# A two-model transformer stack on one core: order of the partial sums in four FFN stages, and one weight place

## The reference

```
def swiglu(x, w_gate, w_up, w_down):
    return (jax.nn.silu(x @ w_gate) * (x @ w_up)) @ w_down
...
    for l in range(DEPTH):
        h = layer_norm(ALPHA * h + 0.5 * swiglu(h, ffn1_w_gate[l], ffn1_w_up[l], ffn1_w_down[l]),
                       ln1_g[l], ln1_b[l])
...
        h = layer_norm(ALPHA * h + 0.5 * swiglu(h, ffn2_w_gate[l], ffn2_w_up[l], ffn2_w_down[l]),
                       ln3_g[l], ln3_b[l])
```

## Time and profile before

| | |
|---|---|
| timed runs, median (lowest to highest) | 1946.63 us (1946.62 to 1950.07), 3 runs |
| profiled execution, span from first to last instruction | 1945.9 us |
| its own time | not given apart from the span |
| TensorE busy | 1931.2 us, 99% |
| VectorE, ScalarE, GpSimd busy | 74%, 52%, 8% |
| DMA | 346.66 MB, mean 178 GB/s |

### The profile page before, as it was taken

How to read it: one execution, slowest core, us unless ns; L and a number is a source line. 1 busy time by engine, 2 the same in 40 slices (tenths; PEclk the granted TensorE clock), 3 DMA queues, 4 the chain that set the end, 5 groups by cost and what they waited for, 6 DMA issues and landing times.

```text
span 1945.9 us, 42335 instructions
## 1 busy us (share of the span) xinstructions
PE 1931.2 (99%) x16150; PEld 1892.7 (97%) x16150; DVE 1431.5 (74%) x2591; ACT 1019.8 (52%) x1527; POOL 152.7 (8%) x192
## 2 busy tenths in 40 slices
PE   9999999999999999999999999999999999999998
PEld 8999989999999999899999999999999999999998
DVE  6774787987588768879978874667765775667763
ACT  4443687554455447865547443665445444565443
POOL 0001123000100011320010100000000000100000
PEclk9999999999999999999999999999999999999999
DMA  7454433545454544345553665445555555435554
GB/s 265 172 197 170 166 109 112 192 174 193 156 192 172 196 164 145 109 152 194 201 191 140 235 233 183 151 149 185 193 214 177 195 202 208 152 131 195 194 213 154
DMA packets 46830, 346.66 MB, mean 178 GB/s; under 512 B 5344, under 2 KB 6416, under 8 KB 9232
## 3 DMA queue, kind: packets, MB, share of 16 engines
q1 hardware_dynamic: 44416, 335.63, 48.0%
q0 software_dynamic: 2320, 9.74, 1.6%
HBM read 344.29 MB, written 1.07 MB: 177 GB/s over the span
## 4 chain that ended last, share of the span: by engine, by line
PE 91%; DVE 4%; ACT 2%; DVEq 1%; issue 1%; DMA 0%; ACTq 0%; SPq 0%; POOL 0%
PE ps L622 22%; PE ps L623 22%; PE ps L624 22%; PE ps L639 14%; PE ps L630 2%; PE ps L631 2%; PE ps L632 2%; DVE w_lo L1996 1%; PE ps L1162 0%; DVE pj L2465 0%; DMA h<-in_hidden 0%; DVE cst L2486 0%; PE ps L1197 0%; DVE pj L2462 0%; ACT scratch L1669 0%
## 5 line engine op out<-in xcount | busy, mean ns | idle before, releaser
L1996 DVE TENSOR_TENSOR w_lo<-raw,w_hi 128x1024 fp32r<-128x1024 f32 (+1 forms) x582 | 749.3, 1313 | 151.1 <-ACT w_hi L1300 91.5
L622 PE MATMUL ps<-x_hi,w_lo 128*128 128x256 f32 (+3 forms) x2208 | 622.1, 282 | 1.5 <-DVE x_lo L2087 0.6
L624 PE MATMUL ps<-x_hi,w_hi 128*128 128x256 f32 (+3 forms) x2208 | 615.1, 279 | 0.0
L623 PE MATMUL ps<-x_lo,w_hi 128*128 128x256 f32 (+3 forms) x2208 | 614.8, 278 | 0.0
L1297 ACT ACTIVATE w_hi<-raw 128x1024 fp32r<-128x1024 f32 x454 | 466.3, 1052 | 92.5 <-PE ps L639 49.0
L622 PE MATMUL ps<-hid_hi,w_lo 128*128 128x256 f32 (+1 forms) x1536 | 431.5, 281 | 0.1
L624 PE MATMUL ps<-hid_hi,w_hi 128*128 128x256 f32 (+1 forms) x1536 | 430.2, 280 | 0.0
L623 PE MATMUL ps<-hid_lo,w_hi 128*128 128x256 f32 (+1 forms) x1536 | 429.8, 280 | 0.0
L622 PEld LDWEIGHTS ps<-x_hi,w_lo 128*128 128x128 f32 x2208 | 414.9, 188 | 6.4 <-issue 4.2
L623 PEld LDWEIGHTS ps<-x_lo,w_hi 128*128 128x128 f32 x2208 | 415.0, 188 | 0.5
L624 PEld LDWEIGHTS ps<-x_hi,w_hi 128*128 128x128 f32 x2208 | 414.6, 188 | 0.0
(11 more groups left out here) (351 smaller groups left out, 2315.3 us busy)
## 6 DMA issues: line engine op xcount, KB each, us to landing
raw<-in_w_up SPq DMA_DIRECT2D x176, 1024.0 KB, 4.8
raw<-in_w_down SPq DMA_DIRECT2D x64, 1408.0 KB, 6.0
raw<-in_w_in SPq DMA_DIRECT2D x36, 1024.0 KB, 4.8
raw<-in_w_out SPq DMA_DIRECT2D x16, 1024.0 KB, 4.8
cst<-row_copy POOLq DMA_DIRECT2D x2, 1088.0 KB, 8.5
raw<-in_w_up SPq DMA_DIRECT2D x4, 512.0 KB, 7.2
cst<-in_consts POOLq DMA_DIRECT2D x1, 1537.5 KB, 6.5
prm<-in_prm POOLq DMA_DIRECT2D x2, 690.0 KB, 7.2
```

Of the source, the lines that this page charges most:

```text
L622: mm(dst, low, xa, start=first, stop=False)
L623: mm(dst, high, xb, start=False, stop=False)
L624: return mm(dst, high, xa, start=False, stop=last)
L1996: v.tensor_tensor(dst, src, high.bitcast(F32), ALU.subtract).then_inc(lo_done, 1)
```

## The change

Three things. In the opening up stage (place OPENING) and in the loops of the second 274-column stage, chunks are summed in the order 0, 2, 4, 6, 1, 3, 5, 7. The second 274-column stage gets a place of its own, SAME_LINE_274, with pitch 8 lines, one line of offset for the high and three for the low buffer, and it sums with `three` rather than `in_pairs`. Down-projections of q = 0 and q = 2 go through the chunks of each half grouped by f modulo four. All other FFNs keep their order.

```diff
+        SAME_LINE_274 = Place(P, LINE, 3 * LINE)
+        EVENS_FIRST = (*range(0, KD, 2), *range(1, KD, 2))
+        BY_LINE = [[f for f in range(u * HALF_F, (u + 1) * HALF_F) if f % 4 == line] for u in range(2) for line in range(4)]
...
-        def level_place(T):
-            return BESIDE_258 if T == T2 else LEVEL_274
+        def level_place(T, q):
+            return BESIDE_258 if T == T2 else SAME_LINE_274 if q == 2 else LEVEL_274
...
-                if T == T1 + 2 and place is not TIGHT:
+                if T == T1 + 2 and place not in (TIGHT, SAME_LINE_274):
                     last = in_pairs(dst, high, low, xa, xb, T)
                 else:
                     step = three_beside if T == T2 + 4 else three
-                    for k in range(KD):
-                        if k in before:
-                            before[k]()
-                        last = step(dst, high[:, k, :], low[:, k, :], xa[:, k, 0:T], xb[:, k, 0:T], k == 0, k == KD - 1)
+                    for n, k in enumerate(EVENS_FIRST if place in (OPENING, SAME_LINE_274) else range(KD)):
+                        if n in before:
+                            before[n]()
+                        last = step(dst, high[:, k, :], low[:, k, :], xa[:, k, 0:T], xb[:, k, 0:T], n == 0, n == KD - 1)
...
-                            for c in range(HALF_F):
-                                f = u * HALF_F + c
-                                col = u * W_WIDE + c * P
+                            order = [f for line in BY_LINE[4 * u:4 * u + 4] for f in line]
+                            if q not in (0, 2):
+                                order = sorted(order)
+                            for f in order:
+                                col = f * P
                                 last = three(ps[:, 4 + j, 0:T], w_hi[:, j, col:col + P], w_lo[:, j, col:col + P],
-                                             ha[:, f, 0:T], hb[:, f, 0:T], f == 0, f == NF - 1)
+                                             ha[:, f, 0:T], hb[:, f, 0:T], f == 0, (u, f) == (1, order[-1]))
```

More of the change, by code:

```diff
@@ L720, in level_up @@
                 N = T + 4 if T == T2 else T + 2
-                xs, place = (plain_hi, plain_lo_of(LEVEL_NORM[norm])), level_place(T)
+                xs, place = (plain_hi, plain_lo_of(LEVEL_NORM[norm])), level_place(T, q)
                 pieces = {5: lambda: mean(norm, T)}
@@ L1503, in unit_hi @@
                     act.wait_ge(unit_used, used)
-                    hi_unit(j, u, width, level_place(T))
+                    hi_unit(j, u, width, level_place(T, q))
                 def pair(it, j, width):
@@ L2192, in pair @@
                     if width == W_NARROW:
-                        lo_unit(turn0 + it + 1, j, 0, width, level_place(T))
+                        lo_unit(turn0 + it + 1, j, 0, width, level_place(T, q))
                     if last:
@@ L2205, in pair @@
                     if width == W_NARROW:
-                        lo_unit(turn0 + it + 1, j, 1, width, level_place(T))
+                        lo_unit(turn0 + it + 1, j, 1, width, level_place(T, q))
                     if last:
```

## The result

The changed kernel takes 1953.18 us (median of 15 timed runs, 1950.54 to 1953.41) against 1947.12 us (15 runs, 1946.50 to 1950.51) for the kernel before; the ratio is 1.0021, 95% interval 1.0014 to 1.0028. It is slower by 0.2%, where the prediction had it 2.9 us faster, and the time lies outside the predicted range of 1937.8 to 1949.6 us.

A forecast was written before the change was run, and what follows sets the result against it. TensorE, busy 1931.2 of 1945.9 us, was taken as the bound, so only matmul pace counts. Opening loop 0, downs -0.3 and second 274-column stage -2.6 gave -2.9 us: median 1943.7 us, range 1937.8 to 1949.6.

The forecast's parts named there:

- Reading: Whole kernel: TensorE busy 1931.2 of 1945.9 us, touched stages full, no wait to remove; only the matmul pace can change.
- Moved place off TensorE, cost 0: Second 274-column stage: ScalarE and VectorE write the weights at pitch 128 floats instead of 160, at cost 0.
- First 274-column loop, 118.3 us: First 274-column loop, not edited: should keep its length of 118.3 us; 120.9 would mean rival 3.
- Rival 3: Both 274-column loops settle badly, first at its twin's pace (+2.6 us), second at the TIGHT row (+1.6); 1950.9 us, chance 0.11.
- Evens first in the opening loop, predicted 0: Opening up-loop, 960 matmuls: same set of weight-to-operand distances, so 0; bounds -3.6 to +1.8 us.
- rival 2: Opening loop, downs, second 274 stage: staying on the same moving line pays, together -7.9 us; 1938.8 us, chance 0.29.
- Downs one and three, predicted -0.3 us: Down-projections one and three: grouping removes most changes between even and odd distances, -0.3 us; bounds -5.3 to +0.6.
- Second 274-column stage, predicted -2.6 us: Second 274-column loop: new order leaves the slow pace 126.0 for 123.3 ns, -2.6 us; bounds -5.0 to +1.6.
- the TIGHT row: Upper bound for the second 274-column loop: three at a time in place TIGHT, 127.7 ns, +1.6 us.
- Even and odd distance: Weights loaded an even number of lines from the moving operand are cheaper: opening loop 123.7, output projection (odd) 125.6 ns.
- Rival 4: Whole change: order and place have no effect or their effects cancel; 1946.6 us, chance 0.18.
- a rule of the Trainium skill: TensorE: separate SBUF read ports for moving operand and weight load, so order and place do nothing; time stays 1946.6 us.

The follow-up runs named there:

- e1: Changed kernel with opening loop and downs one and three back in rising order, down two grouped by line; second 274-column loop 129.24 ns a matmul.
- e12: Kernel before with only the opening loop evens first and downs one and three grouped by line; 1948.40 us, ratio 1.0010.
- e5: Kernel before with opening loop shuffled, down one in steps of two, down three backwards, second 274 loop `three`, plain's low part moved two lines; opening loop 118.78 us.
- e3: Kernel before, rising order, with opening loop in TIGHT, first 274 loop in pairs at pitch 8, second `three` at LEVEL_274; second loop 127.78 ns a matmul.
- e13: Kernel before with high x moved, opening loop in pairs, second 274 loop in pairs at distance 0, all three downs backwards in each half; 1948.27 us, ratio 1.0002.
- e15: Kernel before with the three 272-column downs backwards in each half and second 274 loop in pairs at distance 0; 1948.26 us, ratio 0.9996.
- e8: Kernel before with high x moved, opening and 274 loops in rising pairs at one distance each, downs one and three backwards; opening loop 123.34 ns a matmul.
- e7: Kernel before with opening order 0,2,1,3,4,6,5,7, first 274 loop `three` at Place(8, 1, 1), plain's low part moved two lines; second loop, pairs, 127.79 ns.

## Why the prediction was wrong

**Reading.** TensorE is the bound, the touched stages are full, and the change can act only on the pace: held. No other engine moved.

**Moved place off TensorE, cost 0.** Held: 1221 and 1058 ns.

**First 274-column loop, 118.3 us.** Held: 118.41 by the timeline. Rival 3 rested on this loop falling to its twin's pace, and in the profiled execution it didn't. The loop does have both paces: it was seen at either with the same code ahead of it (before and e1). But the regrouped down one doesn't bring the slow one about (e12), and it isn't why the change lost. Rival 3's other half, the second loop settling dearer with three at a time, did happen, at +2.47 us where it had +1.6. That its time, 1950.9, is near the lower level of the result, 1950.7, is luck: the first half of its sum didn't happen, and the opening loop and the downs, at which it had nothing, cost 1.5 us.

**Evens first in the opening loop, predicted 0.** +1.03 us, inside its bounds of -3.6 to +1.8. The step that failed is "The set is the same": what was kept was the set of distances between weights and moving operand, and what changed was how often the moving line repeats, 0 to 6 times in a sum. There was no row for that. The prediction had noted that staying on a line might have an effect of its own, and gave it the wrong sign (rival 2).

**Downs one and three, predicted -0.3 us.** +0.45. Grouping was to save the changes between even and odd distances; steps of two (e5, down one) leave one change of 10, where grouping leaves three, and gave 124.93. So there was nothing to save but 0.03 ns, and grouping adds repeats, 0.44 ns.

**Second 274-column stage, predicted -2.6 us.** +2.47, beyond even the upper bound of +1.6, and five of the seven us by which the like level (1950.7) misses the forecast. This is the term that decided the sign. Two steps failed. The first is "odds are that it doesn't reproduce the slow one": the loop was given its twin's fast pace although form and place were both new. Every trace with the unchanged code ahead of it entered this loop at 127.8 or, with the moved low part, 127.2, and the fast pace never appeared there. The second is the bound: the TIGHT row, 127.7, was taken as the worst place for `three`, but the new place shares only its pitch. From e3 and e1, form cost +1.77 ns and place +1.46, and evens first gave 0.65 back, which makes the measured 128.59. There was no row of this form in this place, so both ends had to be wider.

**Even and odd distance.** The argument compared two stages (123.7 and 125.6) that differ in more than the distance. e3's opening loop in place TIGHT, the output projection's place, takes 124.44. The output projection, unedited, takes 125.56 in before and 124.43 in after (144 matmuls each): it has two paces of its own, and the row that carried the argument was the slower. The sign holds in that place (124.44 against 123.73), the size was 0.7 ns and not 1.9.

**Rival 2, staying on the line pays.** Refuted in sign where the columns are 272: repeats cost. (Its own terms, -7.9 us, give 1938.7 and not 1938.8.)

**Rival 4, nothing happens.** Refuted: the change cost 4.0 us. Beside it stood a rule of the Trainium skill ("TensorE: Matmul & The Clock Gate", "Step-by-step: what each phase is for"), by which loading the next weights takes nothing from the running matmul. The traces don't agree with what the prediction drew from that rule, that order and place can do nothing: behind one entry, 127.8, 960 matmuls of 274 columns take from 125.56 (e13) to 129.24 ns each (e1) with nothing changed in the loop but place, order and form. Whether it is the load of weights that costs, no run here shows.

**What stays open.** The price of repeats was found at 272 columns only, within one place, and isn't proportional. No rule in lines modulo four that was tried sets the paces at 274. Why the second 274-column loop was never entered fast, what decides between the two entries of the first, where before and e1 have the same code up to there, and why the moved x leaves only the slow one, isn't known. The pace of the output projection ahead doesn't decide it: 125.56 goes with the fast loop in before and with the slow one in e1, 124.43 with the fast in after and with the slow in e15.

## What to carry to other kernels

When one engine is the bound and has no gaps, measure the start-to-start pace of each stage, and test an order or a place by itself on the chip: here form, place and order of one loop were worth +1.77, +1.46 and -0.65 ns, the latter two changed with the sequence in which they were taken, and no rule drawn from other stages of the same trace gave even the signs. An unedited stage seen at two paces in one trace is a warning that a kernel has levels; compare like levels before believing a median, and don't promise a rewritten loop the better of its twin's paces. Reorder a sum only so that no two matmuls in turn start their moving operand on the same line, and even that only for a column count and a place for which it was measured.

## What the runs showed of the hardware

Of the 54 loop paces in the table, half (27) lie on a ladder: 123.34, 124.44, 125.56, 126.68 and 127.79 ns. The step is 1.11 ns, that is 3.33 ns for three matmuls, as long as eight periods of the 2.4 GHz clock that the traces show as granted. It does not follow the columns: 123.34 is the pace of 274 columns in the first loop and of 272 in e8's opening loop. The other half lie off it, among them 123.73, 124.80, 126.01, 128.59 and 129.24, so it is no rule for every loop. The chain of e7 in the second 274-column stage shows one more loop on a rung, pairs with eight repeats:

```profile
545.30 121.78 PE ps L641 x953
```

(121.78 / 953 = 127.8; this piece of the chain covers 953 of the 960 matmuls.) And a pace, once entered, holds. Cut into pieces of 96 matmuls behind the first 96, the loops of all 18 traces stay within 0.3 ns of their mean to the end, with one exception: a piece in the opening loop of after, 0.7 ns dearer, which the same code in e12 doesn't have. The two entries of the same 48 matmuls differ by 1.7 ns. What is read from SBUF in these periods, and what it collides with, the profile doesn't show.
